# A one-layer encoder kernel on eight cores: the last tile's output projections and norms in halves of 256 tokens, a new order of the work, and the scratch copies of branch A written one tile earlier

## The reference

```
h = x @ W_in          # 8 parts of 1024: u, v, q, f, i, og, gA, gB
A:  yA = gelu(u) * (W_s @ layer_norm(gelu(v)) + b)     # in blocks of 128 positions
B:  yB = HGRN2 recurrence over q, f, i in chunks of 64, rms norm, * silu(og)
m   = sig(gA) * (yA @ W_A) + sig(gB) * (yB @ W_B)
x1  = LN(alpha * x + m @ W_o)                          # the first norm
ffn = (gelu(causal_dwconv3(x1 @ W_gate)) * (x1 @ W_val)) @ W_down   # width 2816
e   = sig(x1 @ W_pg) * (p @ W_pp)
out = LN(alpha * x1 + ffn + e)                         # the second norm
```

## Time and profile before

| | |
|---|---|
| median of 3 runs | 2615.2 us (2609.91 to 2616.57) |
| the profiled execution's own time | 2616.36 us |
| its span on the slowest core (core 5) | 2614.8 us |
| spans of the 8 cores | 2585.3 to 2614.8 us |
| PE busy | 2444.9 us, 94% of the span |
| DVE, ACT, POOL busy | 66%, 59%, 8% |
| granted TensorE clock, mean of core 5 | 0.978 of full speed |
| DMA, mean over the span | 165 GB/s, queues of POOL 23.7% and of SP 38.5% of the engines' time |

### The profile page before, as it was taken

How to read it: one execution, slowest core, us unless ns; L and a number is a source line. 1 busy time by engine, 2 the same in 40 slices (tenths; PEclk the granted TensorE clock), 3 DMA queues, 4 the chain that set the end, 5 groups by cost and what they waited for, 6 DMA issues and landing times.

```text
span 2614.8 us, 39128 instructions; the slowest of 8 cores (2585.3 to 2614.8 us)
## 1 busy us (share of the span) xinstructions
PE 2444.9 (94%) x13666; PEld 1245.3 (48%) x13666; DVE 1727.9 (66%) x3043; ACT 1551.8 (59%) x2331; POOL 204.0 (8%) x551
## 2 busy tenths in 40 slices
PE   6989999879998999999999999999999999998797
PEld 3544545434445444454445544454444544454343
DVE  4847765647757577575875768665876768664654
ACT  5856765628746377462875748665685648742452
POOL 2110111001110011100100001000010001000010
PEclk9999999999999999999999999999999999999898
DMA  9998777887885767956444554545455554434343
GB/s 184 210 204 189 154 159 136 196 195 161 187 160 159 215 155 202 193 170 201 142 137 130 185 185 141 154 153 169 154 157 147 160 199 136 135 116 167 110 154 120
DMA packets 119709, 430.19 MB, mean 165 GB/s; under 512 B 13280, under 2 KB 13408, under 8 KB 119520
## 3 DMA queue, kind: packets, MB, share of 16 engines
q1 hardware_dynamic: 92304, 332.52, 38.5%
q0 software_dynamic: 27216, 95.17, 23.7%
HBM read 463.55 MB, written 59.24 MB: 200 GB/s over the span
## 4 chain that ended last, share of the span: by engine, by line
PE 79%; DMA 12%; ACT 5%; DVE 2%; issue 1%; POOL 0%; SPq 0%; ACTq 0%; POOLq 0%; DVEq 0%
PE pg L647 67%; PE pg L872 4%; DMA sb_wsl<-w_in 3%; PE pg L686 3%; DMA sb_wsl<-w_dn 2%; DMA sb_wsl<-scr_wb 1%; ACT sb_xbf L942 1%; DMA sb_wsl<-w_up 1%; DMA sb_xbf<-xT 1%; DMA sb_wsl<-scr_win 1%; PE pg L997 1%; PE pg L739 1%; DMA sb_wsl<-scr_wug 1%; PE pg L765 1%; PE pg L770 0%
## 5 line engine op out<-in xcount | busy, mean ns | idle before, releaser
L647 PE MATMUL pg<-sb_xbf,sb_wsl 128*128 128x512 bf16 x6400 | 1456.3, 382 | 84.9 <-DMA sb_wsl<-w_in 34.8
L647 PEld LDWEIGHTS pg<-sb_xbf,sb_wsl 128*128 128x128 bf16 x6400 | 619.4, 98 | 809.4 <-issue 124.7
L647 PE MATMUL pg<-sb_arena,sb_wsl 128*128 128x512 bf16 x1408 | 311.9, 379 | 6.3 <-DMA sb_wsl<-w_dn 6.3
L647 PEld LDWEIGHTS pg<-sb_arena,sb_wsl 128*128 128x128 bf16 x1408 | 136.2, 98 | 168.3 <-issue 11.0
L917 DVE SCALAR_TENSOR_TENSOR sb_t32a<-sb_t32a,pg 128x512 f32<-128x512 f32 x96 | 65.8, 686 | 221.1 <-PE pg L647 220.3
L971 DVE SCALAR_TENSOR_TENSOR sb_t32b<-sb_gs,sb_cst,sb_t32b 128x512 f32<-128x512 f32 x176 | 131.7, 748 | 84.4 <-ACT sb_t32b L969 83.5
L982 DVE TENSOR_TENSOR sb_arena<-pg,sb_t32b 128x512 bf16<-128x512 f32 x176 | 120.7, 687 | 87.5 <-PE pg L647 80.7
L911 ACT ACTIVATE sb_t32a<-pg 128x512 f32<-128x512 f32 x96 | 57.0, 596 | 202.9 <-PE pg L647 177.6
L965 ACT ACTIVATE sb_gs<-pg 128x512 f32<-128x512 f32 x176 | 104.3, 593 | 91.6 <-PE pg L647 90.8
L966 POOL COPY sb_cy<-sb_gs 128x2 f32<-128x2 f32 x176 | 53.8, 306 | 1316.1 <-ACT sb_gs L965 1316.1
L647 PE MATMUL pg<-sb_yb,sb_wsl 128*128 128x512 bf16 x512 | 127.3, 402 | 27.3 <-DMA sb_wsl<-scr_wb 24.2
(11 more groups left out here) (178 smaller groups left out, 3317.1 us busy)
## 6 DMA issues: line engine op xcount, KB each, us to landing
sb_wsl<-scr_win SPq DMA_DIRECT2D x204, 512.0 KB, 4.1
sb_wsl<-scr_wug SPq DMA_DIRECT2D x66, 512.0 KB, 4.1
sb_wsl<-w_up POOLq DMA_DIRECT2D x55, 512.0 KB, 7.0
sb_wsl<-scr_wuv SPq DMA_DIRECT2D x55, 512.0 KB, 3.8
sb_wsl<-w_in POOLq DMA_DIRECT2D x52, 512.0 KB, 13.7
sb_wsl<-scr_wdn SPq DMA_DIRECT2D x40, 512.0 KB, 3.7
scr_win<-sb_wsl SPq DMA_DIRECT2D x32, 512.0 KB, 11.0
sb_resid<-xT SPq DMA_DIRECT2D x32, 512.0 KB, 5.0
```

What stands on the lines that cost most here:

```text
L647: last = e.matmul(out, lhsT=slot[:, k * 256 + j * 128:k * 256 + (j + 1) * 128], rhs=rhs3[:, k0 + k, :], start=(k0 + k == 0), stop=(k0 + k ...
```

## The change

Five things change.

1. In the last tile (t = 7) the W_o projection, its statistics and its norm run in two halves of 256 tokens, the whole first half being recorded ahead of the second; so do the down projection and the second norm. Each 512-column matmul there becomes two of 256, and each DVE and ACT instruction of these norms two of half the length. The first 6 gate projections of the last tile's b_stage are cut too (SPLIT_G = 6), so that their first halves need only the first half of xbf. The second half of the down projection takes the chunks in the order 4 to 7, 0 to 3 (o = 4) and uses the weights of the last two chunk pairs while they are still in their slots; those of the first two pairs are loaded a second time (6 more loads).
2. In the last tile both norms' statistics are no longer summed by DVE: ACT makes a bf16 copy and a bf16 square of each chunk and PE sums both over the 8 chunks in PSUM with the matrix of 1/1024, 16 matmuls of 256 columns for each half (psum_stats). The copies of the sums (L789, L790) fall away there.
3. In the last tile W_o may use the 5 slots of WR and WH and b_stage all 8; the gate values use 7 buffers in the memory of branch B instead of 2.
4. W_A's scratch copies are written in tile 0 instead of tile 1 ("wa": 0), so tile 1 loads W_A from scratch: 4 cast loads fall away, 4 scratch loads come, and 4 stores move from tile 1 to tile 0. LATE_STORE loses "wb" and "win1", whose copies are then written as soon as the load has landed.
5. The keys and modelled costs of the planner have other values, so that the instruction order of the whole kernel is another.

```
-H_KEY = (-112.695, -25.0, 15.0, 85.167)
-H_SPAN = 40.0
+H_KEY = (-113.718, -25.0, 23.361, 86.994)
+H_SPAN = 40.671
-R_SPAN = 130.0
-U_KEY = -15.728
+R_SPAN = 131.738
+U_KEY = -8.348
+SPLIT_G = 6
+SPLIT_V = 0
+LAST_KEY = 33.675
-DMA_H = 330.0
+DMA_H = 315.951
-DMA_L2 = 1.266
+DMA_L2 = 1.288
-LATE_STORE = ("win5", "wb", "win1", "win0")
+LATE_STORE = ("win5", "win0")
-CAST_TILES = {..., "wa": 1, ...}
+CAST_TILES = {..., "wa": 0, ...}
-FIRST_KEY = 15.0
-FIRST_RATE = 2.0
+FIRST_KEY = -0.864
+FIRST_RATE = 1.845
-MUL_D = 1.0
-SHIFT = (0.0, 3.789, -0.091, 0.0, -0.388, 0.0, -6.384, 0.0, 0.0)
+MUL_D = 0.997
+SHIFT = (-13.917, 2.67, -0.091, 14.256, 6.529, 0.0, -8.179, 0.0, 0.0)
...
+        WL = Union([WR, WH])
+        WL2 = Union([WB, WR, WH])
...
+        def parts(t):
+            return (0, 1) if t == NT - 1 else (None,)
...
+        def psum_stats(dj, h, i):
+            c = span(h)
+            n = TT if h is None else HT
+            if i == 0:
+                sums[h] = (VT(GEN), VT(GEN))
+            for v, f in zip(sums[h], (AF.Copy, AF.Square)):
+                y, Y = BF_.next()
+                fw.act([rbuf(h, dj)], [Y], lambda e, y=y, f=f: e.activation(out=y[:, 0:n], in_=resid[:, dj, c], func=f), n=n)
+                fw.pe([Y, CONSTB], [v], lambda e, v=v, y=y: e.matmul(
+                    v.ap[:, 0:n], lhsT=onesD[:], rhs=y[:, 0:n], start=(i == 0), stop=(i == KC - 1)), n)
...
+            wos = {}
+            for h in parts(t):
+                c = span(h)
+                n = TT if h is None else HT
+                for dp in range(4):
+                    if dp not in wos:
+                        wos[dp] = wload(WR if h is None else WL, f"wo{dp}", w_o[dp], SLOT, t, () if h is None else (gates["wb3", t],))
+                    for j in range(2):
+                        dj = dp * 2 + j
+                        v = proj_h(wos[dp], j, mT, VN, h)
...
+                        stats(dj, TA_, h, 0, t == NT - 1)
+                ln_fin(2, h, t == NT - 1)
+                for dj in range(KC):
+                    ln_chunk(dj, h)
...
+            def proj_s(sl, j, ok):
+                if t < NT - 1 or not ok:
+                    return proj(sl, j, xbf, XB)
+                v = VT(GEN)
+                for h in range(2):
+                    fw.pe([sl] + XH[h], [v], lambda e, v=v, h=h: mm8(e, v.ap[:, span(h)], sl.ap, j, xbf[:, :, span(h)]), HT, 8)
+                return v
...
+            wds = {}
+            for h in parts(t):
+                c = span(h)
+                n = TT if h is None else HT
+                o = 4 if h == 1 else 0
+                for dq in range(4):
+                    dp = (dq + o // 2) % 4
+                    if dq >= 2 or h != 1:
+                        wds[dp] = [(k0, nk, wload(WX, f"wdn{dp}_{k0}", w_dn[dp][:, k0 * 256:(k0 + nk) * 256], nk * 256, t))
+                                   for (k0, nk) in ((0, 8), (8, 8), (16, 6))]
...
+                        stats(dj, TB_, h, o, t == NT - 1)
+                ln_fin(0, h, t == NT - 1)
```

More of the change, by code:

```diff
@@ new lines, in span, with rbuf, rall, xall @@
+        def span(h):
+            return slice(0, TT) if h is None else slice(h * HT, h * HT + HT)
+        def rbuf(h, dj):
+            return R[dj] if h is None else RH[h][dj]
+        def rall(t, dj):
+            return [rbuf(h, dj) for h in parts(t)]
+        def xall(t):
+            return XBs[t % 2] if None in parts(t) else XH[0] + XH[1]
+        def lnb(h):
+            return (ACCY, ACCS, LRS, LNM) if h is None else HALF[h]
+        def own(whole, h, n):
+            return [whole] if h is None else [whole, HALF[h][n]]
@@ new lines, in ln_chunk, with stats @@
+        def ln_chunk(dj, h=None):
+            c = span(h)
+            fw.dve([rbuf(h, dj), lnb(h)[2]], [rbuf(h, dj)], lambda e: e.tensor_tensor(
+                out=resid[:, dj, c], in0=resid[:, dj, c], in1=lnt[:, 0, c], op=ALU.mult), n=TT if h is None else HT)
+        def stats(dj, rot, h=None, o=0, last=False):
+            c = span(h)
+            n = TT if h is None else HT
+            AY, AS = lnb(h)[:2]
+            i = (dj - o) % KC
+            if last:
+                psum_stats(dj, h, i)
+                return
+            if i == 0:
+                fw.act([rbuf(h, dj)], own(ACCS, h, 1), lambda e: e.activation(out=acc[:, 1, c], in_=resid[:, dj, c], func=AF.Square), n=n)
+                return
+            if i == 1:
+                fw.dve([rbuf(h, dj - 1), rbuf(h, dj)], own(ACCY, h, 0), lambda e: e.tensor_tensor(
+                    out=acc[:, 0, c], in0=resid[:, dj - 1, c], in1=resid[:, dj, c], op=ALU.add), n=n)
@@ L819, in sgu_setup @@
+            fw.dve([YS, AS], [AS], lambda e: e.tensor_tensor(out=acc[:, 1, c], in0=acc[:, 1, c], in1=ys[:, 0:n], op=ALU.add), n=n)
         def sgu_setup():
@@ L939, in r_stage @@
-            ln_fin(2)
-            for dj in range(KC):
-                ln_chunk(dj)
-                fw.act([R[dj], CST], [XB[dj]], lambda e, dj=dj: e.activation(
-                    out=xbf[:, dj, :], in_=resid[:, dj, :], func=AF.Identity,
-                    bias=cs("ln1b", dj, 1), scale=cs("ln1g", dj, 1)), ptrs=2)
-            fw.key += 14.0
-            for dj in range(KC):
-                fw.dve([R[dj], LB], [R[dj]], lambda e, dj=dj: e.tensor_scalar(
-                    out=resid[:, dj, :], in0=resid[:, dj, :], scalar1=ag1[:, dj:dj + 1], scalar2=ab1[:, dj:dj + 1],
-                    op0=ALU.mult, op1=ALU.add), n=367)
+            wos = {}
@@ L951, in build @@
+            fw.key += 14.0 if t < NT - 1 else LAST_KEY
+            for h in parts(t):
+                c = span(h)
+                for dj in range(KC):
+                    fw.dve([rbuf(h, dj), LB], [rbuf(h, dj)], lambda e, dj=dj, c=c: e.tensor_scalar(
+                        out=resid[:, dj, c], in0=resid[:, dj, c], scalar1=ag1[:, dj:dj + 1], scalar2=ab1[:, dj:dj + 1],
+                        op0=ALU.mult, op1=ALU.add), n=367 if h is None else 200)
         out_ops = []
+        ft1 = ft[:].rearrange("p a b t -> p (a b t)")
```

146 lines of the change are left out of this document (77 added, 69 removed).

## The result

| | before | after |
|---|---|---|
| median, us | 2612.55 (4 runs) | 2577.19 (4 runs) |
| ratio, 95% interval | | 0.9862 [0.9839, 0.9885] |
| span of the profiled execution's slowest core | 2614.8 | 2581.5 |
| PE busy | 2444.9 | 2448.0 |

The change makes the kernel 1.4% or 36 us faster. I had forecast 14 us and a range that ended at 2586, so the measured time lies outside it.

What follows compares the result with a forecast made beforehand. It took PE's work plus PE's gaps (169.9 us) to bound the kernel. Terms -6.3 - 3.5 - 7 + 3 = -13.8 us took the profiled 2616.36 to 2602.6, so a median of 2601 us against 2615.2, range 2586 to 2612.

Steps and rivals of the forecast that it cites:

- First norm of the last tile: Last tile, first W_o matmul to sixth gate: halves take 36.8 us instead of 43.1, a gain of 6.3 us.
- The term for the clock: Last tile's first norm: 1.7 us for the lower clock, counted at the second halves of the six gates.
- Second norm: Last tile's end: tail falls from 19.1 to 11.9 us; after the price of statistics and halves, a gain of 3.5 us.
- More slots for the last W_o: Last tile's wider weight slots, counted with the new order: no row shows a price, taken as 0 us.
- Tile 0's price: Tile 0: four stores of W_A's copies enter a stretch with full DMA; a loss of 3 us, bounds 0 and 10.
- I take 7, as two slots 2.5 us earlier plus the low clock: Tile 1: without W_A's copies, slots free sooner and low clock is mostly spared; a gain of 7 us, bounds 0 and 15.
- my 4 us for the copies: Tiles 0 and 1: the prediction's term for moving W_A's copies, 7 us gained in tile 1 and 3 lost in tile 0.
- I take 0: Rest of the kernel: the new instruction order changes nothing, 0 us, bounded at some 12 us either way.
- (1): Rival: the new order also closes weight waits in the steady tiles and the last; 12 us more, 2589 us; chance 0.2.
- (2): Rival: the last tile's norms give nothing net, as ACT's queue holds first-half outputs back; 2608 or 2611 us; chance 0.17.
- (3): Rival: tile 0 pays, as W_A's four stores stall cast loads for 30.9 us; 2629 us; chance 0.08.
- One sign of being wrong: Last tile: an ACT queue whose second-half squares stand ahead of first-half outputs; no size given.

Runs made afterwards that it cites:

- e12: Changed kernel with the last tile's W_o back on WR's slots and b_stage on WB's: 175.2 us from W_o to last down matmul, tail 12.1; 16.1 us slower.
- e6: Changed kernel with W_A's copies back in tile 1, all else as changed: ratio to the kernel before 0.9928.
- e2: Kernel before with only W_A's scratch copies moved to tile 0 ("wa": 0): ratio to before 0.9991.
- e3: Kernel before with only the ten new planner constants: ratio to before 0.9954.
- e8: Changed kernel with the old modelled transfer (2.85 us for 512 KB instead of 2.95): tile 3's first W_o matmul at 1206.3 us.
- e18: Repeat of e8, the changed kernel with the old modelled transfer: ratio to before 0.9894.
- e10: Kernel before with only the new SHIFT and R_SPAN: 1214.8 us from tile 3's to tile 7's first W_o matmul, before 1206.0.
- e14: Kernel before with all new planner constants but SHIFT: 1204.8 us from tile 3's to tile 7's first W_o matmul, before 1206.0.
- e1: Changed kernel with the last tile's projections and norms whole again, statistics by DVE: ratio to before 0.9903.
- e4: Halves with their pools and buffers alone: old planner constants, W_A's copies in tile 1, old LATE_STORE; ratio to before 0.9891.

## Why the prediction was wrong

By the table's places the median core gained 37.5 us where the sum had 13.8. Of the 23.7 us between them the halves make 4.3 (14.1 for 9.8), tiles 0 to 3 make 11.6 (15.6 for 4) and the steady tiles 7.7 (for 0).

- **First norm of the last tile: right.** I had 36.8 us from the first W_o matmul to the end of the sixth gate, it is 35.5 (2410.32 to 2445.8, that is 2440.54 and 48 x 0.109); the last half of xbf at 29.9, it is 30.2; idle 7.2, it is 5.1; gain 6.3, it is 7.6. The term for the clock stood at the wrong matmuls: the first halves paid 0.9 us, and the last six statistics matmuls, which I had priced at the full clock, took 1.1 us more than that. ACT was the engine that ended last.
- **Second norm: right, a little small.** Tail 11.9, it is 11.2; price 3.7, it is 3.3 (124.5 us from the sixth gate to the last down matmul against 121.2). Gain 4.6 for 3.5, so 12.2 for 9.8 with the first norm, on the same core. The prices taken for halves held: DVE took 0.42 us for my 0.46 (0.61 of the whole's 0.683, where I had said two thirds, by interpolation), ACT 0.40 for 0.41, and no second table load stood ahead of the second half's Ln. The formula of **VectorE: DVE Perf Modes** (The TRN2 errata) in the Trainium skill gave 0.42, which the trace now bears out to 0.01.
- **"More slots for the last W_o" at no price: wrong, though it didn't move the sum.** I named DMA's rate as the cover of the six more loads. The rate was enough; slots weren't. Without the wide pools the halves give nothing (e12). A 256-column matmul takes 0.109 us against 0.216, so a half uses up its weights in half the time. That the pool was the cover is shown by e12 as a whole; which of its two pools, and how much through the new order, is not.
- **Tile 0's price: mis-sized.** +3, it is +7.1 at W_o 0. e6 puts 8.6 us on the copies, in the new order; in the old order e2 has 1.1.
- **"I take 7, as two slots 2.5 us earlier plus the low clock": the step that failed most.** W_o 0 to W_o 1 fell by 19.3 us. The slot was held as I read (POOL's waits on the copy are gone after, and back in e6). What failed is the size: I read it from the stalls of the old order, as a term that adds to the others, with a bound of 15. Net of tile 0, my 4 us for the copies are 1.0 us over e2's executions and 13.8 over e6's against the changed kernel's; in tile 1 alone the traces have 11 and 25. So the rows of the old order did not price the copies for the new one.
- **"I take 0" for the new order: wrong.** It gave 7.7 us in the steady tiles, and 8.8 over the whole in e3's executions, alone; in tiles 0 to 3 the plan with the old modelled transfer is 10 or more slower (e8, e18). Both signs were open by the traces, and I said so. Two waits on W_B with 2.1 and 2.4 us and slow matmuls behind them stood in the rows, 4.0 us for the second, but e10 and e14 lose them without the gain: which of PE's many short gaps the order closed was not to be read from a single wait.
- **The rivals.** (1) came nearest: the order gave more, on top of the forecast; I gave it 0.2 and 12 us, and tiles 0 to 3 and the steady tiles together were some 19 us over their terms. Its mechanism came true in part only: the waits on W_B in tiles 4 and 5 went, those on weights ahead of the last W_o projection stayed (9.4 us before, 10.4 after), and much of the 19 us is the copies in the new order. (2) is refuted by e1 and e4, (3) by the W_o 1 column: tile 0 loses 7 us and nothing stalls behind it for good.
- Of the signs: no gap over 8 us, a tail under 13 us, no POOL wait on the copy in tile 1 came true; PE's idle time in 480 to 600 us is 9.0 us, below my 14. New waits on weights above 5 us at 180 to 300 us: none. One sign of being wrong came true in part, and cost little: the second half's first copies and squares on ACT (L833, from 2425.32) stand between outputs of the first half (L1014, from 2426.26). The mechanism of the halves was right; the range failed since it bounded the order by 12 us and the copies by their own waits, and had no term for the two together.

## What to carry to other kernels

Halving the last tile's columns hides a norm behind its own projections when nothing else is left to hide it, and here the gain could be worked out from rows of the kernel before to a quarter (9.8 us for 12.2 on the same core); but check what every half consumes twice as fast, here weight slots. Where an instruction order comes from a planner, the parts of a change don't add: each edit turns the plan over (the copies gave 1.0 us in the old order and 13.8 in the new one), and a plan made with a modelled transfer 0.1 us shorter lost as much as the edit under study gave. A range for such a change has to be wide enough for the parts together, and one wait that goes away is no proof of where the gain came from: look for a run that lost the wait too.

## What the runs showed of the hardware that I had not expected

- Behind a gap of 2.37 us, with PE busy up to it, the granted clock was 0.61 and then 0.74 (1778.9 to 1784.0 us, before): the next two groups of 8 took 2.84 and 2.30 us instead of 1.73, so the wait cost 4.0 us in all.
- The cores of one chip, with the same program, reach W_o of tile 3 at 1181.2 to 1211.4 us in one execution of the changed kernel (core 6 and core 5), and nearly keep their distance from there on (2089.4 and 2120.2 at W_o of tile 6). The cores end in nearly the order in which they reach W_o 3, so which is the slowest was settled in tiles 0 to 3 of this execution, where the DMA share in tile 0's merge is 1.01 of the engines' time.
